# A decoder layer on one core: w_out and value products spread over more heads, the first up chunk converted within the attention, the MoBA keys turned later

## The chip, the cores and the metric

The kernel runs on one core of one Trainium2 chip. The metric is the device time of one execution in microseconds; the profile's span leaves out a little at its ends. TensorE (PE) multiplies and transposes, PEld is its weight load, VectorE (DVE), ScalarE (ACT) and GpSimd (POOL) do the elementwise work, and SyncE (SP) issues nearly all DMAs. Each engine executes its own instructions in order and waits on semaphores.

## What is computed

One layer on 512 tokens of width 1024, all float32:

```
u = rms_norm(x);  proj = u @ w_in            # 416 latent columns, then q, k, v of MoBA, 512 each
MLA:  8 heads, q and k of 64 + 32 rotary, v of 64, from low-rank latents, causal softmax
MoBA: 8 heads of 64, rotary q and k; own block of 256 keys causal, past blocks by top-3 gate
mix = [MLA heads, MoBA heads];  h = x + rms_norm(mix @ w_out) * g
a = square(relu(rms_norm(h) @ w_up))         # 4096 wide
out = h + rms_norm(a @ w_down) * g
```

With two blocks in all, MoBA's selection takes every past block, so its heads are plain causal attention too.

## The kernel before, in words

**Precision.** Every matrix product is made of float32r parts: an operand is split into a high part (ScalarE, `hi_part`, L439) and a low part (VectorE, `lo_part` L710 or with a gain `lo_scaled` L713), and `mm3` (L1029) issues three matmuls: high x high, high x low, low x high. A weight chunk of 1 MB lands in one of two `raw` slots, ScalarE writes its high part, VectorE its low part; `w_ready` counts the finished chunks. Chunks are numbered: 0 to 9 for the input side, 10 to 13 for w_out (`OUT_CH`), 14 and 15 the first two of w_up (`UP_CH`), and so on. SP asks for a chunk when the one two before it has been converted (`chunk`, L248). w_out's chunks are converted in pieces of 512 columns (`out_piece`): the high part by ScalarE (L585), the low part by GpSimd (L380), and four of the sixteen low parts by VectorE (L894).

**Stages.** The input projection goes by column groups of w_in: latents, MoBA q, MoBA k. Its third group (L1185) already holds the transposes for heads 0 and 1 and the scores of head 0. Then comes the loop over 16 heads in `for i in range(NH + 2)`, written out on each of four engines. In step i, TensorE (L1261) computes the scores of head i, makes the first filler (`filler(i, 0)`), the weighted sum of head i-2, transposes the probabilities of head i-1 (`first_T`), makes the second filler, a query or key transpose for a later head, and the rest of the transposes (`last_T`). A filler is two of a unit's `mm3`: the MoBA values (steps 0 to 7, `V_HALVES`), and the half of w_out's product that goes over the MLA rows (steps 10 to 17, `OUT_UNITS`); steps 8 and 9 have none. All use bank 5, which ScalarE empties (`v_part` L576, `out_part` L580) into v_moba or y_part.

Per head the other engines do this. VectorE takes four row maxima (`maxes`, L844), ScalarE the exponentials with their sums (`exps`, L548), VectorE two reciprocals (`inverse_sums`, L856), GpSimd multiplies the probabilities by them (L407 to L411, "normalizing"), TensorE transposes, ScalarE and VectorE split the transposed probabilities in three parts (`p_part`, banks 3, 4 and 3 again), and after the weighted sum ScalarE copies and VectorE adds the two halves of a head (`o_part`). GpSimd splits the sum of each pair of heads (`split_pair`, L387). Of the queries, head i+2's is transposed in step i (`Q_LATE`), a pair of keys in steps 1, 3 and 5 (`K_EARLY`), both for MoBA in steps 6, 8, 10, 12 (`MOBA_PREP`), all in bank 7 (`PREP`). The keys of MoBA are turned (rotary) by VectorE (`swapped` L790, two multiplications of 256 columns; `turned` L804, one of 512) and GpSimd (`rope_add` L366) in step 0: two tiles before the maxima of head 0, two behind. Step 0 ends for ScalarE and VectorE with weight chunk 9 (`in_hi(7)`, `in_lo(7)`).

w_out's pieces stand in steps 6 to 9 (`OUT_PIECES`, L229): on ScalarE and VectorE before `o_part`, on GpSimd at the start of the next step, before the normalizing.

**Behind the heads.** TensorE computes the rest of w_out's product (L1289 to L1312): four token tiles of two halves, 32 `mm3`; then it transposes tile after tile of the new rows and multiplies with w_up in halves of the tokens (L1323 to L1336). ScalarE and VectorE first convert the two up chunks (L643 to L646, L946), which SP asked for behind the four h rows and the gain (L291 to L296). Then, tile by tile, VectorE adds y_part (`added`, L949), ScalarE takes squares, GpSimd the root, VectorE scales and adds the residual (`scaled`, L958), and the transposed rows are split (`transposed_lo`, L728).

The few lines that set the order on SP:

```
L291  sp.wait_ge(o_full, NH)
L292  for t in range(NT):
L293      sp.dma_start(h_sb[:, t, :], x_v[t]).then_inc(h_in[t], 16)
L294  sp.dma_start(post_g[:, :], attn_post_g.to_broadcast([P, D])).then_inc(g_post_in, 16)
L295  for j in range(2):
L296      chunk(UP_CH + j, w_up_v[:, :, 256 * j:256 * j + 256], CW)
```

## Time and profile before

| | |
|---|---|
| median of 3 runs | 642.06 us (641.32 to 642.21) |
| profiled execution, its own time | 643.8 us |
| its span | 641.9 us |
| TensorE busy | 599.7 us, 93% |
| VectorE busy | 309.7 us, 48% |
| ScalarE busy | 281.8 us, 44% |
| GpSimd busy | 113.1 us, 18% |
| chain that ended last | TensorE 81%, VectorE 7%, ScalarE 6%, DMA 2% |
| mean granted TensorE clock | 0.966 |

The page says where time goes by engine. Matmuls overlap and their ends are modelled, so the busy time of TensorE is a little generous: the distance between the starts of two matmuls tells its pace. Three parts follow each other on the time axis: the input projection up to about 92 us, the heads up to 239 us, the transition to the MLP up to 295 us, and the MLP.

### The profile page before, as it was taken

The numbers are of one execution on the slowest core, as the hardware profiler recorded it, in microseconds if no ns is written. First come the engines' busy times: TensorE is split into PE (matmuls) and PEld (weight loads), VectorE is DVE, ScalarE is ACT, GpSimd is POOL, SyncE is SP. The second block draws the span as 40 slices with busy tenths as digits, with TensorE's granted clock in tenths as the row PEclk, the third lists the DMA queues.
The fourth block names the chain that finished last, engine by engine and source line by source line (L and its number), as shares of the span: only waits on it lengthen the run. The fifth ranks groups of instructions, "written<-read, shape, count | busy, mean of one in ns | idle before, by whom it ended". The sixth has DMA issues, their size and how long they took to land.

```text
span 641.9 us, 8151 instructions
## 1 busy us (share of the span) xinstructions
PE 599.7 (93%) x2916; PEld 506.1 (79%) x2916; DVE 309.7 (48%) x596; ACT 281.8 (44%) x581; POOL 113.1 (18%) x173
## 2 busy tenths in 40 slices
PE   8999998998699989369999999999999999999996
PEld 7989877886578877269888888888888888888885
DVE  4478486776656531762543443434242323242435
ACT  5746445667746643236442435353323131322232
POOL 1414153448744520112000000000000000000001
PEclk9999997999679999679999999999999999999999
DMA  8414311001200017400323233332332323222203
GB/s 307 115 61 140 123 66 65 2 1 65 67 0 1 2 36 260 131 1 1 102 94 110 86 98 98 87 109 74 124 131 66 123 73 105 91 92 104 98 1 131
DMA packets 32828, 55.24 MB, mean 86 GB/s; under 512 B 3233, under 2 KB 21409, under 8 KB 32801
## 3 DMA queue, kind: packets, MB, share of 16 engines
q1 hardware_dynamic: 31760, 54.90, 25.7%
q8 instruction: 15, 0.25, 0.2%
q10 hardware_dynamic: 1040, 0.00, 0.1%
q14 instruction: 13, 0.10, 0.0%
HBM read 52.80 MB, written 2.10 MB: 86 GB/s over the span
## 4 chain that ended last, share of the span: by engine, by line
PE 81%; DVE 7%; ACT 6%; DMA 2%; issue 2%; SPq 1%; POOL 0%; DVEq 0%; POOLq 0%; ACTq 0%
PE bank L1031 25%; PE bank L1033 24%; PE bank L1032 24%; PE bank L1190 2%; DVE w_lo L714 2%; ACT probs L557 2%; DMA w_raw<-in_w_up 2%; ACT w_hi L440 1%; PE bank L1224 1%; PE bank L1223 1%; DMA x_sb<-in_x 1%; DVE pT_lo L711 1%; ACT junk_post L465 1%; PE bank L1133 1%; DVE un L964 1%
## 5 line engine op out<-in xcount | busy, mean ns | idle before, releaser
L1031 PE MATMUL bank<-uT_hi,w_hi 128*128 128x512 f32 (+1 forms) x280 | 105.3, 376 | 5.1 <-DVE uT_lo L711 5.1
L1032 PE MATMUL bank<-uT_lo,w_hi 128*128 128x512 f32 (+1 forms) x280 | 105.0, 375 | 0.0
L1033 PE MATMUL bank<-uT_hi,w_lo 128*128 128x512 f32 (+1 forms) x280 | 105.0, 375 | 0.0
L1031 PE MATMUL bank<-w_hi,a_hi 128*128 128x512 f32 x256 | 99.8, 390 | 0.1
L1033 PE MATMUL bank<-w_hi,a_lo 128*128 128x512 f32 x256 | 99.7, 390 | 0.0
L1032 PE MATMUL bank<-w_lo,a_hi 128*128 128x512 f32 x256 | 99.7, 390 | 0.0
L711 DVE TENSOR_TENSOR w_lo<-w_raw,w_hi 128x2048 fp32r<-128x2048 f32 (+2 forms) x21 | 42.6, 2036 | 106.6 <-ACT w_hi L440 106.6
L440 ACT ACTIVATE w_hi<-w_raw 128x2048 fp32r<-128x2048 f32 (+2 forms) x25 | 36.5, 1490 | 111.7 <-PE bank L1033 110.9
L714 DVE SCALAR_TENSOR_TENSOR w_lo<-w_raw,g_up,w_hi 128x256 fp32r<-128x256 f32 x128 | 52.0, 481 | 46.6 <-ACT w_hi L440 46.6
L341 POOL TENSOR_SCALAR stat<-stat 128x1 f32<-128x1 f32 x8 | 1.7, 218 | 374.6 <-ACT junk_post L465 374.6
L1031 PEld LDWEIGHTS bank<-uT_hi,w_hi 128*128 128x128 f32 x280 | 53.8, 192 | 14.4 <-issue 5.5
L675 ACT ACTIVATE relu<-bank 128x512 f32<-128x512 f32 x32 | 19.1, 598 | 98.2 <-PE bank L1033 98.2
L1032 PEld LDWEIGHTS bank<-uT_lo,w_hi 128*128 128x128 f32 x280 | 53.9, 192 | 9.0
L1033 PEld LDWEIGHTS bank<-uT_hi,w_lo 128*128 128x128 f32 x280 | 53.9, 192 | 9.0
L1031 PE MATMUL bank<-w_hi,uT_hi 128*128 128x512 f32 (+1 forms) x144 | 57.8, 402 | 0.6 <-DVE v_moba L890 0.4
L440 ACT ACTIVATE w_hi<-w_raw,g_up 128x256 fp32r<-128x256 f32 x128 | 52.6, 497 | 10.8 <-DMA w_raw<-in_w_up 10.8
L410 POOL TENSOR_TENSOR probs<-probs,rs 128x512 f32<-128x512 f32 (+1 forms) x64 | 46.8, 753 | 56.1 <-DVE rs L862 56.1
L1031 PEld LDWEIGHTS bank<-w_hi,a_hi 128*128 128x128 f32 x256 | 48.1, 188 | 10.5 <-issue 0.5
L1032 PEld LDWEIGHTS bank<-w_lo,a_hi 128*128 128x128 f32 x256 | 48.1, 188 | 10.0
L1033 PEld LDWEIGHTS bank<-w_hi,a_lo 128*128 128x128 f32 x256 | 48.1, 188 | 9.8
L1033 PE MATMUL bank<-w_hi,uT_lo 128*128 128x512 f32 (+1 forms) x144 | 55.6, 386 | 0.0
L1032 PE MATMUL bank<-w_lo,uT_hi 128*128 128x512 f32 (+1 forms) x144 | 55.5, 386 | 0.0
(149 smaller groups left out, 968.3 us busy)
## 6 DMA issues: line engine op xcount, KB each, us to landing
w_raw<-in_w_up SPq DMA_DIRECT2D x16, 1024.0 KB, 5.3
w_raw<-in_w_down SPq DMA_DIRECT2D x16, 1024.0 KB, 4.8
w_raw<-in_w_in SPq DMA_DIRECT2D x6, 1024.0 KB, 5.8
w_raw<-in_w_out SPq DMA_DIRECT2D x4, 1024.0 KB, 4.9
x_sb<-in_x SPq DMA_DIRECT2D x8, 256.0 KB, 6.0
h_sb<-in_x SPq DMA_DIRECT2D x4, 512.0 KB, 5.5
out<-h_sb SPq DMA_DIRECT2D x8, 256.0 KB, 2.0
w_raw<-in_w_in SPq DMA_DIRECT2D x2, 416.0 KB, 5.2
```

Source lines behind the costliest of these rows:

```text
L410: nc.gpsimd.tensor_tensor(pr, pr, rs[:, i % 2, t:t + 1].to_broadcast([P, P * (t + 1)]), ALU.mult).then_inc(s_norm, 1)
L440: return nc.scalar.activation(out, whole, ACT.Copy, scale=scale)
L465: nc.scalar.activation(junk[:, 0:src.shape[1]], src, ACT.Square, scale=scale, accum_out=stat[:, norm, t, col:col + 1]).then_inc(sq, 1)
L557: nc.scalar.activation(probs[i % 2][:, p_off(t):p_off(t) + n], ps[b][:, c:c + n], ACT.Exp, bias=nb[:, i % 2, t:t + 1], scale=-1.0, accum_o ...
L675: nc.scalar.activation(relu[:, m, :], ps[2 * j + m][:, :], ACT.Relu).then_inc(relu_c, 1)
L711: return nc.vector.tensor_tensor(out, whole, hi.bitcast(F32), ALU.subtract)
L714: return nc.vector.scalar_tensor_tensor(out=out, in0=whole, scalar=scale, in1=hi.bitcast(F32), op0=ALU.mult, op1=ALU.subtract)
L964: nc.vector.scalar_tensor_tensor(out=y, in0=y, scalar=stat[:, 3, t, 3:4], in1=post_g[:, w], op0=ALU.mult, op1=ALU.mult).then_inc(y_s, 1)
L1031: nc.tensor.matmul(out, lh, rh, start=start, stop=False)
L1032: nc.tensor.matmul(out, lh, rl, start=False, stop=False)
L1033: return nc.tensor.matmul(out, ll, rh, start=False, stop=stop)
L1190: last = nc.tensor.transpose(ps[b][:, c + P * (t - k):c + P * (t - k) + P], probs[i % 2][:, p_off(t) + P * k:p_off(t) + P * k + P], ident[ ...
```

## The change

- **Fillers.** The sixteen quarters of the value units stand at both halves of steps 0 to 5, then at (6, 1), (7, 1), (8, 1) and (9, 0); those of w_out's units from (10, 1) to (17, 1), and one behind the loop. A quarter is two `mm3`. ScalarE empties w_out's units between the second and the third exponential of a head (`OUT_DONE`).
- **Pieces of w_out.** ScalarE's stand in steps 5, 6, 8 and 9, VectorE's in 8 and 9, both at the end of the step; GpSimd's stand behind the normalizing in steps 6, 7 and 9, and two at the start of step 10.
- **First up chunk.** It has tiles of its own, `up0_hi` and `up0_lo`, where the natural MoBA queries and keys were. SP asks for both up chunks before the h rows. ScalarE and VectorE convert the first in four pairs of 256 columns at the ends of steps 13 to 16; the second is converted behind the heads, as before.
- **Query of head 2.** Transposed in the projection's third group, in bank 3; before it was step 0's late query in bank 7. The key part of heads 2 and 3 waits for ScalarE's copies of bank 7 instead of that query.
- **Turning of the MoBA keys.** One tile in each of steps 1 to 4: the swap between the two reciprocals, the multiplication behind them, GpSimd's addition behind the normalizing. `rt2` has a place of its own.
- **After the heads.** VectorE adds tiles 0 and 1 before it scales tile 0, and so on. `o_part` stays before the probabilities' split ("the sum still ahead of the next transposes").

The diff, cut to what the prediction speaks of:

```diff
-        Q_LATE = {i: i + 2 for i in range(HEADS - 2)}
+        Q_LATE = {i: i + 2 for i in range(1, HEADS - 2)}
-        V_HALVES = range(0, 2 * NT)
-        OUT_UNITS = range(NH + 2 - 2 * NT, NH + 2)
+        V_AT = {(i, half): 2 * i + half for i in range(6) for half in range(2)}
+        V_AT.update({(6, 1): 12, (7, 1): 13, (8, 1): 14, (9, 0): 15})
+        V_DONE = {2: 0, 4: 1, 6: 2, 10: 3}
+        OUT_AT = {((u + 21) // 2, (u + 21) % 2): u for u in range(4 * NT - 1)}
+        OUT_DONE = {11 + u: u for u in range(2 * NT - 1)}
+        TURNED = {1 + t: NT + t for t in range(NT)}
-        OUT_PIECES = {6 + c: [PIECES * c + n for n in range(PIECES)] for c in range(4)}
+        OUT_PIECES = {i: [PIECES * c + n for n in range(PIECES)] for c, i in enumerate((5, 6, 8, 9))}
         DVE_PIECES = {8: (8, 9), 9: (12, 13)}
+        POOL_PIECES = {6: (0, 1, 2, 3), 7: (4, 5, 6, 7), 9: (10, 11), 10: (14, 15)}
+        UP0_PIECES = {13 + n: (2 * n, 2 * n + 1) for n in range(4)}
...
+            for j in range(2):
+                chunk(UP_CH + j, w_up_v[:, :, 256 * j:256 * j + 256], CW)
+
             sp.wait_ge(o_full, NH)
             for t in range(NT):
                 sp.dma_start(h_sb[:, t, :], x_v[t]).then_inc(h_in[t], 16)
             sp.dma_start(post_g[:, :], attn_post_g.to_broadcast([P, D])).then_inc(g_post_in, 16)
-            for j in range(2):
-                chunk(UP_CH + j, w_up_v[:, :, 256 * j:256 * j + 256], CW)
...
             for i in range(NH + 1):
+                for n in POOL_PIECES.get(i, ()) if i == 10 else ():
+                    out_piece(n)
                 if i >= 4 and i % 2 == 0:
                     split_pair(i // 2 - 2)
-                for n in OUT_PIECES.get(i - 1, []):
-                    if n not in DVE_PIECES.get(i - 1, ()):
-                        out_piece(n)
...
+                if i in TURNED:
+                    rope_add(TURNED[i])
+                for n in POOL_PIECES.get(i, ()) if i != 10 else ():
+                    out_piece(n)
...
                 if i < NH:
-                    exps(i, S_ORDER)
+                    exps(i, S_ORDER[:2])
+                if i in OUT_DONE:
+                    out_part(OUT_DONE[i])
+                if i < NH:
+                    exps(i, S_ORDER[2:])
                 if i == 0:
+                    q_part(2, 3)
                     natural(NT + 2)
...
-                for n in OUT_PIECES.get(i, []):
-                    out_piece(n)
                 if i >= 2:
                     o_part(i - 2)
...
+                for n in OUT_PIECES.get(i, []):
+                    out_piece(n)
+                if i in UP0_PIECES:
+                    up0_pieces(UP0_PIECES[i])
...
-            for j in range(2):
-                act.wait_ge(*SLOT_LEFT[UP_CH + j][0])
-                mlp_hi(j, UP_CH + j)
+            act.wait_ge(*SLOT_LEFT[UP_CH + 1][0])
+            mlp_hi(1, UP_CH + 1)
...
-                if i == 0:
-                    turn_two(NT)
...
                     maxes(i, S_ORDER)
-                    inverse_sums(i)
+                    inverse_sums(i, 0)
+                    if i in TURNED:
+                        swapped(TURNED[i])
+                    inverse_sums(i, 1)
                 if i == 0:
-                    turn_two(NT + 2)
+                    q_part(2, 3)
                     in_lo(7)
+                if i in TURNED:
+                    turned(TURNED[i])
...
-            for j in range(2):
-                mlp_lo(j, UP_CH + j)
+            mlp_lo(1, UP_CH + 1)
...
+            added(0)
+            added(1)
+            dve.wait_ge(g_post_in, 16)
+            post_norm(0)
+            added(2)
+            post_norm(1)
+            transposed_lo(2 * NT, 0)
+            transposed_lo(2 * NT, 1)
+            added(3)
+            post_norm(2)
+            post_norm(3)
+            transposed_lo(2 * NT, 2)
+            transposed_lo(2 * NT, 3)
...
+                elif (part, t) == (1, 3):
+                    pe.wait_ge(qup_c, 2 * NT)
+                    q_prep(2, 3)
...
                 if i in K_EARLY:
-                    pe.wait_ge(ql, i + 2)
+                    pe.wait_ge(*((nat_c, 2 * NT) if i == 1 else (ql, i + 2)))
                     k_prep(K_EARLY[i], PREP)
...
-            pe.wait_ge(w_ready, UP_CH + 2 - NO)
+            pe.wait_ge(w_ready, UP_CH + 1 - NO)
             pe.wait_ge(ul, 2 * NT + 4)
-            up_block(0, 0, 0, A)
+            up_block(0, 0, 0, A, (up0_hi, up0_lo))
...
+            pe.wait_ge(w_ready, UP_CH + 2 - NO)
             up_block(2, 1, 0, A)
```

## Rows read from the trace of the kernel before

**Rows 1.** The page's slices of 16 us: TensorE's busy tenths, and its granted clock.

```profile
PE   8999998998699989369999999999999999999996
...
PEclk9999997999679999679999999999999999999999
```

**Rows 2.** Windows, one per step: length, busy us (count) by engine, granted clock, DMA, GB/s.

```profile
92.68:105.53 12.85, 9.67 (x44) 7.93 (x42) 9.72 (x19) 5.28 (x14) 5.61 (x6) 0.73 0.24 82
...
130.15:138.94 8.79, 8.33 (x53) 7.19 (x50) 6.02 (x17) 6.33 (x16) 3.63 (x6) 1.00 0.00 0
138.94:148.70 9.76, 8.11 (x53) 7.06 (x51) 6.28 (x18) 7.83 (x19) 6.59 (x8) 1.00 0.01 2
148.70:157.42 8.72, 7.39 (x44) 6.17 (x44) 5.07 (x16) 6.27 (x17) 6.04 (x8) 1.00 0.35 120
157.42:167.70 10.28, 6.15 (x40) 4.87 (x39) 8.30 (x20) 7.82 (x19) 10.28 (x10) 0.86 0.31 102
167.70:178.09 10.39, 8.20 (x32) 6.87 (x31) 6.65 (x17) 6.38 (x16) 6.33 (x8) 0.64 0.01 3
178.09:189.46 11.37, 11.37 (x51) 9.53 (x51) 5.41 (x16) 4.90 (x14) 6.14 (x7) 0.70 0.00 0
189.46:196.92 7.46, 7.46 (x44) 6.12 (x43) 4.83 (x15) 5.05 (x14) 3.69 (x6) 1.00 0.00 0
196.92:205.13 8.21, 8.21 (x52) 7.02 (x51) 5.38 (x16) 5.38 (x15) 3.75 (x5) 1.00 0.01 2
```

**Rows 3.** Windows of the idle time in step 8 and of the stretch behind the heads.

```profile
163.90:167.08 3.18, 0.26 (x4) 0.02 (x2) 3.18 (x5) 3.05 (x6) 3.18 (x5) 0.65 0.85 267
239.17:295.02 55.85, 38.78 (x201) 33.71 (x200) 27.44 (x50) 19.50 (x45) 4.77 (x14) 0.85 0.36 121
255.50:267.14 11.64, 0.15 (x1) 0.00 (x1) 9.46 (x22) 3.74 (x10) 1.01 (x3) 0.71 0.58 180
```

**Rows 4.** Timelines behind the heads (start, us, what, idle before); the h rows' landing.

```profile
251.30 6.50 ACT L440 ACTIVATE w_hi<-w_raw,g_up 128x256 fp32r<-128x256 f32 x16 [10.82 <-DMA w_raw<-in_w_up]
...
254.64 6.45 DVE L714 SCALAR_TENSOR_TENSOR w_lo<-w_raw,g_up,w_hi 128x256 fp32r<-128x256 f32 x16 [13.43 <-ACT w_hi L440]
261.00 1.28 DVE L956 TENSOR_TENSOR un<-bank,y_part 128x512 f32<-128x512 f32 x2
264.47 1.41 DVE L964 SCALAR_TENSOR_TENSOR un<-un,stat,post_g 128x512 f32<-128x512 f32 x2 [2.18 <-POOL stat L345]
265.80 1.29 DVE L969 TENSOR_TENSOR h_sb<-un,h_sb 128x512 f32<-128x512 f32 x2
...
DMA to landing us min/median/max: 4.3/5.5/6.2
```

**Rows 5.** Timelines of VectorE and TensorE at the start of the heads.

```profile
80.07 2.74 DVE L714 SCALAR_TENSOR_TENSOR w_lo<-w_raw,g_in,w_hi 128x512 fp32r<-128x512 f32 x4 [1.65 <-ACT w_hi L440]
82.73 1.43 DVE L799 TENSOR_TENSOR rt<-mk_nat,rope_sb 128x256 f32<-128x256 f32 x4
...
88.84 1.31 DVE L799 TENSOR_TENSOR rt<-mk_nat,rope_sb 128x256 f32<-128x256 f32 x2 [0.40 <-ACT mk_nat L440]
...
92.97 4.39 DVE L714 SCALAR_TENSOR_TENSOR w_lo<-w_raw,g_in,w_hi 128x512 fp32r<-128x512 f32 x4 [0.32 <-ACT w_hi L440]
...
98.02 0.80 PE L1031 MATMUL bank<-cT_hi,wkv_hi 128*128 128x512 f32 x1 [3.18 <-DVE qT_lo L711]
```

**Rows 6.** GpSimd's forms by cost, a row of ScalarE's timeline, and waits within the heads.

```profile
L410 POOL TENSOR_TENSOR probs<-probs,rs 128x512 f32<-128x512 f32 x15 | 15.6, 1041 | 53.0 <-DVE rs L862 53.0
...
L385 POOL TENSOR_TENSOR wo_lo<-w_raw,wo_hi 128x512 fp32r<-128x512 f32 x8 | 10.0, 1276 | 0.0
...
144.28 2.21 ACT L440 ACTIVATE wo_hi<-w_raw 128x512 fp32r<-128x512 f32 x4
...
DVE rs L862 <- ACT probs L557: 16.4, 15, 1.1
...
PE bank L1031 <- ACT y_part L583: 2.2, 2, 1.1
```

More of the change, by code:

```diff
@@ L590, in out_piece, with up0_pieces @@
                 hi_part(out_tiles(c)[0][:, w], raw[OUT_CH[c] % 2][:, w]).then_inc(wo_hi_ready, 1)
+            def up0_pieces(pair):
+                if pair[0] == 0:
+                    act.wait_ge(g_up_in, 16)
+                    arrived(UP_CH)
+                for k in pair:
+                    w = slice(256 * k, 256 * k + 256)
+                    last = hi_part(up0_hi[:, w], raw[UP_CH % 2][:, w], g_up[:, k:k + 1])
+                last.then_inc(up0_h, 1)
             k_part(0, 0)
@@ L932, in _ @@
                     k_part(MOBA_PREP[i], PREP)
+                for n in DVE_PIECES.get(i, ()):
+                    out_piece(n)
+                if i in UP0_PIECES:
+                    up0_pieces(UP0_PIECES[i])
             dve.wait_ge(last_h, 1)
@@ L1287, in _ @@
                     last_T(i - 1)
+            out_quarter(4 * NT - 1)
             def out_final(t, b, ks):
```

139 lines of the change are left out of this document (65 added, 74 removed).

## The prediction

> **What bounds the kernel now.** First the page's slices: of 40, TensorE is at nine tenths or more in all but eight; the low ones are slices 7, 10, 11, 15, 17 and 18 (16 us each), and the granted clock is down in 7, 11, 12, 17 and 18 [rows 1]. Behind them the MLP keeps TensorE busy up to the last slice. TensorE's work is the same in both kernels, so the change is worth what it takes out of those dips. I call "step i" the stretch from the first score matmul of head i to that of head i+1. By step [rows 2], a step in which TensorE never idles takes 7.46 us (head 11) or 8.21 us (head 12, with a query and a key transposed as well). Heads 1 and 6 to 10 take far longer: 12.85, 9.76, 8.72, 10.28, 10.39 and 11.37, three of them at a granted clock of 0.64 to 0.86. Near the end of the heads TensorE waits twice for the copy of y_part, 1.1 us each [rows 6]. Then the attention is over at 239.17 and the stretch up to the end of the first three part blocks of the MLP (295.02) takes 55.85 us [rows 3]. Its work is 32 products of 0.683 us (three matmuls of 512 columns at 0.2275 from start to start), four groups of transposes of 0.81 and three half blocks of 2.95: 33.9 us. 11.64 us of the difference are idle in one piece [rows 3].
>
> Times behind the heads count from the end of the last filler, T0 = 239.17.
>
> **The transition, after T0.** Before, VectorE gets both up chunks first: ScalarE waits 10.82 us for the DMA and converts from 251.30 to 257.8, VectorE ends at 261.09, and only then adds tile 0, at T0+21.8, though its 8 products had been ready at T0+5.5 (8 x 0.683) [rows 4]. After, the DMA sits inside the attention, one chunk is converted there, and one remains: ScalarE T0+0.7 to +4.0 (half of 6.50), VectorE +4.0 to +7.2 (half of 6.45). On SP's queue the two chunks move ahead of the h rows and wait there for raw slots that GpSimd's and VectorE's w_out pieces free, in my walk by the middle of the heads; so they block nothing, and the h rows are asked for after the last weighted sum, as before. Those landed in 4.3 to 6.2 us [rows 4], the gain behind them a little later, so all by about T0+9, before the first norm at +12.2. Now each step of VectorE, with durations of [rows 4]:
> - Sum 0 (1.28): +7.2 to 8.5. Its norm could start at +10.7, 2.2 after the sum (ScalarE's squares, GpSimd's root). Sum 1 needs tile 1's products (T0+10.9): ends +12.2. Norm 0 (1.41+1.29, together 2.62) ends +14.9. TensorE is in tile 2 until +16.4 and finds the rows for the transposes ready.
> - Sum 2 ends +17.0, norm 1 +19.6; TensorE wants it at +20.0 after half of tile 3. No wait.
> - TensorE ends tile 3 at +23.5 (32 x 0.683 + 2 x 0.81). The low parts of tiles 0 and 1 are ready at about +22.5. First block to +26.5. Sum 3 ends +24.1, norm 2 +26.7: a wait of 0.3. Then transposes, block, transposes, block, with norm 3 at +29.4, ready: end at +34.2.
> So 55.85 becomes 34.2: **21.6 us**. The order "sum 1 before norm 0" makes norm 0 1.5 us later; that is hidden under tile 2's products, and costs 1.5 if they end early. The first block needs only the chunk from the heads, so the second chunk's conversion hides under all of tiles 0 to 3. TensorE's new wait for the second chunk stands before the third block, 24 us after it is ready.
>
> **The start, heads 0 to 5.** In step 1 before, TensorE idles 3.18 us up to 98.02 because it waits for head 2's query in bank 7; VectorE has turned four tiles of the MoBA keys and then took 4.39 us for a chunk that took 2.74 at 80.07 [rows 5]. After, the query is transposed and split during the projection. The key part of head 2 waits for the natural copies alone, ready at 90.7. The filler's second weight chunk: ScalarE 90.7 to 93.2, VectorE 2.74 more, 95.95; TensorE gets there at 95.5, an idle time of 0.5, and the clock has no reason to fall. It was at 99.47 before and then ran at half (matmuls 0.43 us apart instead of 0.23). New is this: VectorE has maxes (1.8), a turn (1.4), key parts (1.39) and the probabilities' low part between that and the transposes of head 0, and TensorE waits about 1.8 us before the late query. Scores of head 2 then start at 102.3 instead of 105.53: **3.2 us**. In heads 2 to 5 the turn of one tile per head costs VectorE 2 x 0.36 and one more of 512 columns, about as much: 1.4 us [rows 5], put into two waits it has anyway: 1.1 us for the exponentials before the second reciprocal, [rows 6] and that for the key's high part behind them. GpSimd's additions (1.46 us each) stand behind its normalizing, where it waits some 3 us for the next head. If the cover were gone, four turns would cost 5.6 us. Steps 3 and 5 stay at 8.8 us, step 2 and 4 at 7.7: 0.4 us more.
> Against it speaks that the turn reads two SBUF tiles while GpSimd normalizes. The row: with GpSimd at work the pair of multiplications took 1.31 us instead of 0.72 (half of 1.43), and the chunk 4.39 instead of 2.74 [rows 5]. From +0.2 to +0.6 for a pair and as much for the other multiplication, partly hidden: I take 1.0 us off for all four heads, bounds 0 and 3.
> If instead each of the three VectorE operations of a turn waited out one of GpSimd (1.04 us the longest [rows 6]), four heads would lose 3 x 1.04 x 4 = 12.5 us: the second rival. The Trainium skill ("SBUF — State Buffer", section "SBUF: two separate sides") states that rule: VectorE with two SBUF inputs and GpSimd share a port pair by an exclusive lock for a whole instruction. The trace shows it only in part.
>
> **Heads 6 to 11.** Before, heads 8 and 9 have no filler, and ScalarE does four pieces of w_out (2.2 us) ahead of the sum and the probabilities, GpSimd four (4 x 1.276 = 5.1 us) ahead of the normalizing [rows 6]. TensorE waits for all of them, and the clock halves: by the means of 0.86, 0.64 and 0.70 in steps 8, 9 and 10, for about 2.9 + 7.5 + 6.8 = 17 us [rows 2]. Half of that, 8.6 us, is lost where TensorE had work. After, every one of heads 6 to 10 has one quarter (1.4 us), and pieces come last. My walk by the durations of these steps, with head 6 at 0 (before: 9.76, 18.48, 28.76, 39.15, 50.52 for heads 7 to 11, 57.98 for head 12):
> - Step 6: the pieces of head 5 hold the last third of the probabilities back by about 1.5, TensorE waits for the queries' low part; 9.2.
> - Step 7: pieces of head 6 in the same place; 8.0. TensorE has one transposing pair and 1.4 us of filler less than in a full step, so ScalarE binds: 1.2 (last third) after the scores, maxes, exponentials 2.15, sum 0.6 and 0.7, low part 0.6, transposes, back to the scores.
> - Step 8: nothing in the way; TensorE's own work, 6.6.
> - Step 9: pieces of head 8 on ScalarE, two on VectorE; TensorE idle 2.7; 9.1.
> - Step 10: the same from head 9, v_moba's last tile too; 9.3. GpSimd, with 5.0 + 1.9 + 5.0 ahead, ends the normalizing 3.6 us before TensorE needs it.
> - Step 11: 7.4.
> Sum 49.6 instead of 57.98: **8.4 us**.
>
> **Heads 12 to the end.** The two waits of 1.1 to 1.3 for the copy of y_part go, since half a step now lies between a unit and the next: 2.6. One quarter more is left to do: -1.4. Two pieces of the up chunk per head 13 to 16 take ScalarE 0.95 and VectorE 0.8, most of it in ScalarE's 0.9 us of waiting for the last third of the transposes; -0.5 for four, bounds 0 and 2. **0.7 us**.
>
> **Sum.** 3.2 + 0.4 - 1.0 + 8.4 + 0.7 = 11.7, and 21.6: 33.3 us. The profiled execution took 643.8, so 610.5; the runs' median (642.06) is 1.7 lower, and so is my forecast: **608.8**. The MLP behind has TensorE without idle time before and should keep it. What a measurement of this kernel can tell from no change is about 0.2% (1.3 us).
>
> **Rivals.**
> - *Clock falls once or twice in steps 9 to 11.* Before, TensorE was idle 3.18 us up to 98.02 and nearly so from 163.90 to 167.08, and its clock was down in both places [rows 3, 5]; mine are 2.7 and at most 1.8. One stretch of some 7 to 10 us at the lower level (1.2 GHz) costs half its length where TensorE is full: 612 to 614. Chance 0.23.
> - *The turns pay the full price of GpSimd's operations*: 12.5 instead of 1.0, 620.3. It decides once turns outgrow their 2 us of cover; then VectorE binds steps 1 to 4. For it: VectorE's pair went from 0.72 to 1.31 beside GpSimd. Against it: the chunk of four operations was stretched by 1.65 and not by four times 1.04 [rows 5], and VectorE is busy for 6.0 of 8.8 us in step 5 [rows 2], which leaves room. 0.08.
> - *The early chunks do nothing*, because slot 1 comes free late or the sums stay chained behind the conversion; 642.1 - 11.7 = 630.4. Against it: the last out piece is done by head 10. 0.04.
> - *Slower.* One quarter per head is so little that TensorE's clock stays at half from head 6 to the last head. There TensorE has some 83 us of work at full clock; at half it takes 75 us more than my 91: about 684. It decides from the point where the halved stretches hold over 67 us of matmuls. Against it: step 7 with TensorE busy for 7.39 of 8.72 us kept a clock of 1.00 [rows 2]. 0.03.
> The forecast itself: 0.60, its own range 605.5 to 612; 0.02 for what is none of these. The range leaves out the last three: 604.5 to 615. Faster 0.96, same 0.01, slower 0.03.
>
> **What would show it.** Right: no idle of 11 us behind the last head, the sums start some 7 us after it; the stretch of 55.85 is under 36. Scores of head 2 near 102, of head 12 near 186; the first half-clock stretch of the attention gone. Wrong: granted clock below 1 in steps 9 to 11; turns of over 2 us beside GpSimd; a wait of ScalarE for the up chunk; TensorE waiting for h_sb before its last transposes.

## The result, and the profile after

The changed kernel takes 618.29 us (median of 4 runs, 617.81 to 618.97), the kernel before 641.79 beside it (641.32 to 642.21). The ratio is 0.9635, with an interval of 0.9618 to 0.9651. The forecast was 608.8 with a range of 604.5 to 615.0: the direction was right, the size was not, and the time lies 3.3 us above the range. Of the 33.3 us that the steps promised, 23.5 came by the medians and 26.0 by the profiled executions (643.8 to 617.81; its span 616.0). The execution of before that was profiled was one of its long ones: all runs of that kernel in this study lie between 640.1 and 645.0, those of the changed one between 617.5 and 619.0.

The page's slices of the changed kernel, now 15.4 us each, TensorE's busy tenths and its granted clock:

```profile
PE   7999998998799999999999999999999999999996
...
PEclk9999999997969999999999999999999999999999
```

Five slices are under nine tenths, the first, 7, 10, 11 and the last, where [rows 1] had eight; the clock is down in 10 and 12 alone. The deep dips, of 3 and 6 tenths behind the heads and of 6 in steps 8 and 9, are gone.

The windows by step (columns as in [rows 2]), from step 1 to the end of the last filler, and last the stretch up to the end of the first three part blocks:

```profile
92.88:102.61 9.73, 7.49 (x43) 5.75 (x41) 9.04 (x21) 5.16 (x15) 3.98 (x5) 1.00 0.29 108
...
127.00:135.82 8.82, 8.33 (x53) 7.19 (x50) 6.17 (x18) 6.42 (x17) 4.85 (x7) 1.00 0.00 0
135.82:145.08 9.26, 7.22 (x46) 5.88 (x46) 6.28 (x18) 7.67 (x20) 4.51 (x6) 1.00 0.01 2
145.08:154.06 8.98, 8.98 (x39) 8.08 (x38) 5.44 (x16) 6.29 (x17) 8.32 (x9) 0.62 0.32 117
154.06:161.12 7.06, 7.06 (x45) 5.87 (x44) 4.96 (x15) 5.12 (x14) 3.78 (x4) 1.00 0.28 85
161.12:172.95 11.83, 7.57 (x38) 5.95 (x37) 6.38 (x18) 7.11 (x19) 7.84 (x11) 0.85 0.11 41
172.95:182.78 9.83, 9.83 (x46) 8.44 (x45) 8.39 (x19) 6.82 (x18) 9.75 (x10) 0.66 0.65 209
182.78:190.55 7.77, 7.62 (x43) 6.11 (x42) 4.87 (x16) 5.16 (x14) 3.31 (x6) 1.00 0.01 5
...
206.86:214.95 8.09, 7.62 (x43) 6.12 (x42) 6.07 (x17) 5.38 (x16) 4.43 (x6) 1.00 0.00 0
...
234.56:269.17 34.61, 34.17 (x201) 30.04 (x200) 23.58 (x41) 15.80 (x36) 8.10 (x14) 1.00 0.35 122
```

Steps 2 and 4 and steps 3 and 5 are alike, so 127.00 stands for step 5; head 12 starts at 190.55, and T0 is 234.56. Where the time went, against the forecast:

| stretch | before | forecast | after |
|---|---|---|---|
| head 6's first score | 138.94 | 2.6 less | 135.82, 3.1 less |
| steps 6 to 11 | 57.98 | 49.6 | 54.73 |
| head 12 to T0 | 42.25 | 0.7 less | 44.01 |
| T0 to three part blocks | 55.85 | 34.2 | 34.61 |
| from there to the end of the span | 346.9 | the same | 346.8 |

The two ends are right within half a microsecond; 7.6 us are missing in the middle, of which 5.1 in steps 6 to 11 and 2.5 from head 12 on. The stretch of steps 6 to 11 has the clock at half for as long as before, 17 us: 6.8 in step 7 (from 145.4) and 10.2 in steps 9 and 10 (from 169.3). The fall in step 1 is gone.

VectorE's timeline behind T0 (columns as in [rows 4]):

```profile
238.58 3.25 DVE L733 SCALAR_TENSOR_TENSOR w_lo<-w_raw,g_up,w_hi 128x256 fp32r<-128x256 f32 x8 [3.94 <-ACT w_hi L448]
241.75 1.88 DVE L985 TENSOR_TENSOR un<-bank,y_part 128x512 f32<-128x512 f32 x3
245.64 0.69 DVE L985 TENSOR_TENSOR un<-bank,y_part 128x512 f32<-128x512 f32 x1 [2.01 <-PE bank L1069]
246.25 1.40 DVE L993 SCALAR_TENSOR_TENSOR un<-un,stat,post_g 128x512 f32<-128x512 f32 x2
```

VectorE finishes the second chunk and adds tile 0 at T0+7.2, where [rows 4] had T0+21.8, and scales it at +11.7. The second half of tile 1 waits 2.01 us for its products, so what sets the time is TensorE's products, as the forecast had it.

Then GpSimd's and TensorE's timelines around step 9:

```profile
165.03 0.61 POOL L403 CAST uT_hi<-o_sum 128x512 fp32r<-128x512 f32 x1 [7.19 <-PE bank L1069]
...
166.94 5.45 POOL L417 TENSOR_TENSOR probs<-probs,rs 128x512 f32<-128x512 f32 x8
...
169.74 1.54 PE L1229 MATMUL bank<-ident,probs 128*128 128x128 f32 x6 [3.65 <-POOL probs L417]
```

GpSimd stands idle for 7.19 us, and what it waits for is a matmul. Then it normalizes heads 8 and 9 back to back (8 tiles), and TensorE idles 3.65 us until it has done so. The second half of step 8, with nothing in GpSimd's hands to do, is where head 8's normalizing should have been. `split_pair(2)` (L401) waits not only for the sum of its heads but for all four value units, since for the third pair the split goes over rows that the value fillers still read:

```
pool.wait_ge(*((qup, 2 * NT) if c < 2 else (proj, 4 * NT)))
```

The change moved the last value quarter to (9, 0), into the step behind the one in which GpSimd asks for it. Behind that instruction stands the normalizing of head 8, for which TensorE waits.

Last, rows of VectorE's and GpSimd's timelines that show single prices:

```profile
98.01 1.59 DVE L818 TENSOR_TENSOR rt<-mk_nat,rope_sb 128x256 f32<-128x256 f32 x2
...
113.85 0.74 DVE L818 TENSOR_TENSOR rt<-mk_nat,rope_sb 128x256 f32<-128x256 f32 x2
...
206.95 1.90 DVE L733 SCALAR_TENSOR_TENSOR up_lo<-w_raw,g_up,up_hi 128x256 fp32r<-128x256 f32 x2
...
215.12 0.88 DVE L733 SCALAR_TENSOR_TENSOR up_lo<-w_raw,g_up,up_hi 128x256 fp32r<-128x256 f32 x2
...
207.08 1.49 POOL L405 TENSOR_TENSOR uT_lo<-o_sum,uT_hi 128x512 fp32r<-128x512 f32 x1
```

A turn's swap beside GpSimd takes 1.59 us against 0.74 where it starts ahead of GpSimd's operation (113.85 against 114.01); an up piece pair takes 1.90 beside GpSimd's split and 0.88 otherwise.

### The profile page after: what moved, and what is told of

Same layout as the page of the kernel before. It is cut to its first block, busy times and chain, and to the rows that moved or that the text cites. A ratio compares the mean times of both kernels' runs of the same rounds, so it can differ in the third digit from the quotient of the medians.

```text
span 616.0 us, 8166 instructions
## 1 busy us (share of the span) xinstructions
PE 593.9 (96%) x2916; PEld 499.8 (81%) x2916; DVE 310.7 (50%) x596; ACT 282.5 (46%) x581; POOL 116.5 (19%) x173
## 4 chain that ended last, share of the span: by engine, by line
PE 86%; DVE 5%; ACT 4%; issue 2%; DMA 1%; POOL 1%; SPq 0%; DVEq 0%; POOLq 0%; ACTq 0%
PE bank L1067 27%; PE bank L1069 26%; PE bank L1068 26%; PE bank L1229 2%; ACT probs L565 2%; DVE pT_lo L730 1%; PE bank L1263 1%; PE bank L1262 1%; DMA x_sb<-in_x 1%; PE bank L1169 1%; DVE w_lo L733 1%; DVE o_sum L902 1%; ACT w_hi L448 1%; PE bank L1073 1%; PE bank L1109 1%
## 5 line engine op out<-in xcount | busy, mean ns | idle before, releaser
L1067 PE MATMUL bank<-uT_hi,w_hi 128*128 128x512 f32 (+1 forms) x248 | 94.9, 383 | 0.0
L1068 PE MATMUL bank<-uT_lo,w_hi 128*128 128x512 f32 (+1 forms) x248 | 94.8, 382 | 0.0
L1069 PE MATMUL bank<-uT_hi,w_lo 128*128 128x512 f32 (+1 forms) x248 | 94.8, 382 | 0.0
L733 DVE SCALAR_TENSOR_TENSOR w_lo<-w_raw,g_up,w_hi 128x256 fp32r<-128x256 f32 x120 | 48.8, 480 | 37.1 <-ACT w_hi L448 37.1
L1024 DVE TENSOR_TENSOR act_sb<-relu 128x512 f32 (+1 forms) x32 | 22.1, 689 | 64.6 <-ACT relu L694 64.6
L1069 PEld LDWEIGHTS bank<-uT_hi,w_lo 128*128 128x128 f32 x248 | 46.6, 188 | 9.1
L1067 PEld LDWEIGHTS bank<-uT_hi,w_hi 128*128 128x128 f32 x248 | 46.6, 188 | 9.1
L1068 PEld LDWEIGHTS bank<-uT_lo,w_hi 128*128 128x128 f32 x248 | 46.6, 188 | 8.9
```

Of the source, the lines that this page charges most:

```text
L733: return nc.vector.scalar_tensor_tensor(out=out, in0=whole, scalar=scale, in1=hi.bitcast(F32), op0=ALU.mult, op1=ALU.subtract)
L1024: nc.vector.tensor_tensor(act_sb[:, bass.ds(i * 4 + (2 * j + m), 1), :], relu[:, m:m + 1, :], relu[:, m:m + 1, :], ALU.mult).then_inc(a_re ...
L1067: nc.tensor.matmul(out, lh, rh, start=start, stop=False)
L1068: nc.tensor.matmul(out, lh, rl, start=False, stop=False)
L1069: return nc.tensor.matmul(out, ll, rh, start=False, stop=stop)
```

## The experiments

Three questions were open. First, whether the loss in steps 6 to 11 is the wait of `split_pair(2)`, or whether the clock falls there by itself, because the steps hold too little work for TensorE. Second, what the conversion of the up chunk costs in the heads, and what it buys. Third, how much of the gain each of the forecast's parts really is. Each kernel below is the changed kernel with one edit, if nothing else is said; ratios are to the kernel before, timed beside it. One thing bears on several of the comparisons: in the profiled executions of the changed kernel step 7 takes 8.98 us, with a fall of the clock, and in those of the first, third, fourth, fifth and sixth variant below it takes 8.20, without one, though their edits touch nothing that this step waits for. Of their differences from the changed kernel 0.8 us is therefore owed to no edit, as far as the profiled execution stands for the others.

### The split behind the normalizing

```diff
-                if i >= 4 and i % 2 == 0:
+                if i >= 4 and i % 2 == 0 and i != 8:
                     split_pair(i // 2 - 2)
...
+                if i == 8:
+                    split_pair(2)
```

> The changed kernel, with GpSimd's split of the third pair of heads put behind the normalizing of head 8 instead of ahead of it. Theory A (in the changed kernel GpSimd waits 7.2 us at that split, for the last value quarter in step 9, and head 8's normalizing stands behind it; TensorE then idles 3.65 us for it and the clock halves): the idle time goes, step 9 falls from 11.8 to about 9 and step 10 from 9.8 to about 9.0, the clock stays at 1.00 in both; 613.5 to 615 us. Rival B (step 9 is long because ScalarE's and VectorE's w_out pieces of step 8 hold back the last third of head 7's probabilities): step 9 stays near 11.8 and the time at 618. Rival C (the clock falls because steps 6 to 10 have too little work): the idle time goes but the clock still reads below 1 in steps 9 or 10; 616 us.

Measured: 614.58 us (614.52 to 614.91), 0.9563 (0.9537 to 0.9589), 3.7 less than the changed kernel. GpSimd's timeline, of this kernel:

```profile
157.73 2.76 POOL L417 TENSOR_TENSOR probs<-probs,rs 128x512 f32<-128x512 f32 x4
164.17 0.61 POOL L403 CAST uT_hi<-o_sum 128x512 fp32r<-128x512 f32 x1 [3.68 <-PE bank L1071]
...
166.09 2.75 POOL L417 TENSOR_TENSOR probs<-probs,rs 128x512 f32<-128x512 f32 x4
```

Head 8 is normalized at 157.73, ahead of the wait, and head 9 at 166.09. The wait itself, still 3.68 us, stands behind work that is done. The windows of steps 9 and 10:

```profile
160.28:168.75 8.47, 6.23 (x37) 5.11 (x37) 6.29 (x18) 7.21 (x19) 4.71 (x7) 1.00 0.21 85
168.75:179.44 10.69, 9.73 (x46) 8.11 (x45) 9.10 (x19) 6.61 (x18) 10.49 (x11) 0.68 0.61 196
```

Step 9 falls from 11.83 to 8.47. But step 10 rises from 9.83 to 10.69: there the clock is at half for 6.8 us from 170.2. So the wait is the cause of the loss in step 9. It is worth 2.5 us in steps 9 and 10 together (21.66 to 19.16); most of the rest of the 3.7 is the 0.8 of step 7. What is left of a low clock has another cause.

### All value fillers before step 8

The values go back to both halves of steps 0 to 7, as before, w_out's to steps 10 to 17, and the copy of each unit ahead of all exponentials of a head.

```diff
-        V_AT = {(i, half): 2 * i + half for i in range(6) for half in range(2)}
-        V_AT.update({(6, 1): 12, (7, 1): 13, (8, 1): 14, (9, 0): 15})
-        V_DONE = {2: 0, 4: 1, 6: 2, 10: 3}
-        OUT_AT = {((u + 21) // 2, (u + 21) % 2): u for u in range(4 * NT - 1)}
+        V_AT = {(i, half): 2 * i + half for i in range(8) for half in range(2)}
+        V_DONE = {2: 0, 4: 1, 6: 2, 8: 3}
+        OUT_AT = {((u + 20) // 2, (u + 20) % 2): u for u in range(4 * NT)}
```

> The changed kernel with the fillers where they were (values in steps 0 to 7, w_out from step 10 on, none in 8 and 9, each unit emptied ahead of the exponentials); the pieces, the early chunk, the early query and the turns stay changed. Theory A: the values are done in step 7, so the split of the third pair does not wait and head 8's normalizing is early, but TensorE has no filler in steps 8 and 9: it idles there and the clock may halve; steps 12 to 17 come back to 7.46 us with two waits of 1.1 at the end. I expect 616 to 620, so the spreading is worth next to nothing. If spreading is worth what I forecast (about 5 us of the 8.4 in steps 6 to 11): 622 to 624.

Measured: 615.36 us (614.07 to 618.27), 0.9567 (0.9537 to 0.9597). Windows of steps 8 to 11 of this kernel, with edges within 0.1 us of the steps' own:

```profile
156.40:165.30 8.90, 8.76 (x39) 7.61 (x38) 5.71 (x17) 5.74 (x15) 8.82 (x10) 0.62 0.36 118
165.30:173.70 8.40, 4.95 (x31) 3.97 (x30) 6.48 (x18) 7.13 (x19) 3.41 (x6) 1.00 0.01 4
173.70:185.10 11.40, 11.40 (x52) 9.56 (x51) 7.99 (x18) 6.05 (x17) 9.97 (x10) 0.70 0.57 184
185.10:192.50 7.40, 7.40 (x43) 6.07 (x42) 4.82 (x15) 5.01 (x14) 3.67 (x6) 1.00 0.00 0
```

Here GpSimd's split has no value filler to wait for. Steps 8 and 10 run at 0.62 and 0.70, and yet the kernel is 2.9 us faster than the changed one, and only 0.8 slower than the one with the split behind, which has its fillers spread. So the fillers over more heads brought 0.8 us at most, which the two intervals cannot tell from nothing, and they made the wait. (The profiled execution is the longest of the four, 618.27; it has a fall of the clock in step 2, which takes 10.59 us instead of 7.78.) With the copy ahead of the exponentials steps 11 to 13 take 7.46, 8.23 and 7.46 us, as in the kernel before, and 7.77, 8.55 and 7.76 in the changed one: the copy between the exponentials costs 0.3 us in each. The pieces stand as in the changed kernel, and steps 7 to 11 take 45.0 us against 48.2 [rows 2]: that gain comes without the spread fillers.

### The first up chunk behind the heads

```diff
-                if i in UP0_PIECES:
-                    up0_pieces(UP0_PIECES[i])
...
+            for pair in UP0_PIECES.values():
+                up0_pieces(pair)
```

The same on ScalarE and VectorE, ahead of the second chunk.

> The changed kernel with the first up chunk converted behind the heads, after the last split of the sums and ahead of the second chunk; both are still asked for before the h rows. Theory: ScalarE and VectorE take 3.3 us more each before sum 0, so sum 0 starts at about +10.5 instead of +7.2, norm 0 ends at about +16 to +17 (sum 0, sum 1 at +13, norm 0), about when TensorE reaches its transposes (+16.4), norm 1 at +21 to +22 against the +20.0 TensorE wants it: 1 to 3 us lost, and about 1 us won in steps 14 to 16. 618 to 621. Rival: the early conversion is what gave the 21 us: 628 or more.

Measured: 616.50 us (616.32 to 616.66), 0.9592 (0.9565 to 0.9618): 1.8 us faster than the changed kernel. VectorE's timeline behind T0 (232.31), of this kernel:

```profile
233.93 3.28 DVE L733 SCALAR_TENSOR_TENSOR up_lo<-w_raw,g_up,up_hi 128x256 fp32r<-128x256 f32 x8 [1.54 <-ACT up_hi L448]
239.53 3.26 DVE L733 SCALAR_TENSOR_TENSOR w_lo<-w_raw,g_up,w_hi 128x256 fp32r<-128x256 f32 x8 [2.32 <-ACT w_hi L448]
```

And its windows, from head 15 to T0 and from there to the three part blocks:

```profile
214.12:232.31 18.19, 18.04 (x100) 15.18 (x99) 8.82 (x22) 9.62 (x22) 4.64 (x6) 1.00 0.09 30
232.31:266.90 34.59, 34.09 (x198) 29.50 (x197) 26.77 (x49) 18.60 (x44) 7.42 (x14) 1.00 0.35 122
```

The transition is nearly as long as in the changed kernel, though VectorE has both chunks to do, because TensorE has 32 products to make meanwhile. The first block starts 24.0 us behind T0 instead of 23.6 and the third at 32.0 instead of 31.7; the window's edge at 266.90 lies 0.4 us ahead of the end of the third. Step 14 and what follows up to T0 take 1.84 us less (25.87 against 27.70). So converting the chunk within the heads costs 1.8 us and buys 0.4. That the whole run gains 1.8 and not 1.4 fits the shorter step 7.

### The chunks asked for behind the h rows

The edit before, and SP asks for the up chunks where the kernel before did:

```diff
             sp.dma_start(post_g[:, :], attn_post_g.to_broadcast([P, D])).then_inc(g_post_in, 16)
+            for j in range(2):
+                chunk(UP_CH + j, w_up_v[:, :, 256 * j:256 * j + 256], CW)
```

> The kernel with the first chunk converted behind the heads (e3_chunk_behind), and with both up chunks asked for behind the h rows and the gain, as before. Theory D (the gain of the transition comes from the earlier request: the 10.8 us that ScalarE waits for the DMA): the first chunk lands near +12, both are converted by +22, sum 0 starts there as in the kernel before; TensorE idles 10 us ahead of its transposes and the clock falls; 12 to 15 us more than e3_chunk_behind, 628 to 632. Rival (the new order of sums and norms hides most of it): 620 to 623.

Measured: 628.34 us (627.18 to 629.27), 0.9766 (0.9747 to 0.9784), 11.8 more than the kernel above. Timelines of ScalarE and VectorE, of this kernel (T0 is 234.07):

```profile
244.35 3.31 ACT L447 ACTIVATE up_hi<-w_raw,g_up 128x256 fp32r<-128x256 f32 x8 [9.49 <-DMA w_raw<-in_w_up]
...
250.90 3.25 DVE L732 SCALAR_TENSOR_TENSOR w_lo<-w_raw,g_up,w_hi 128x256 fp32r<-128x256 f32 x8 [2.32 <-ACT w_hi L447]
254.07 2.48 DVE L984 TENSOR_TENSOR un<-bank,y_part 128x512 f32<-128x512 f32 x4
```

ScalarE waits 9.49 us for the DMA, VectorE is through with the chunks 20 us behind T0, and TensorE's first part block starts at +35.2 instead of +24.0. By the profiled executions 10.8 us of the difference lie behind T0 and 1.2 in step 2, where the clock falls and which the edit does not touch. The earlier request alone is worth some 11 us.

### Norms in turn

```diff
-            added(0)
-            added(1)
-            dve.wait_ge(g_post_in, 16)
-            post_norm(0)
-            added(2)
-            post_norm(1)
...
+            for t in range(NT):
+                added(t)
+                if t == 0:
+                    dve.wait_ge(g_post_in, 16)
+                if t >= 2:
+                    transposed_lo(2 * NT, t - 2)
+                post_norm(t)
+            for t in range(2, NT):
+                transposed_lo(2 * NT, t)
```

> The changed kernel with VectorE's order behind the heads as before: sum, norm, sum, norm, with the low parts of tiles 0 and 1 behind sums 2 and 3. Theory (the order matters, because the first up block waits for the low parts of tile 1, which then stand behind sum 3): sum 0 at +7.2, norm 1 ends at +19.4, norm 2 at +25.5, low part of tile 1 at about +28; the first block starts there instead of at +23.6, so 4 to 5 us more, 622 to 623.5. Rival (all of the transition's gain comes from the earlier chunks, the order is free, as the forecast's text had it for sum 1 and norm 0): 618 to 619.

Measured: 623.48 us (623.11 to 623.79), 0.9693 (0.9677 to 0.9709), 5.2 more than the changed kernel. VectorE's timeline, of this kernel (T0 is 234.98):

```profile
258.14 1.41 DVE L993 SCALAR_TENSOR_TENSOR un<-un,stat,post_g 128x512 f32<-128x512 f32 x2
...
260.67 1.28 DVE L985 TENSOR_TENSOR un<-bank,y_part 128x512 f32<-128x512 f32 x2
261.87 1.28 DVE L730 TENSOR_TENSOR uT_lo<-bank,uT_hi 128x512 fp32r<-128x512 f32 x2
```

The low part of tile 1, which the first part block needs, stands behind the sum of tile 3 at 261.87. The first block starts at +28.3 instead of +23.6, and the clock falls for 3.4 us at 263.2. The order of the sums is worth 5 us.

### The turning of the keys in step 0

```diff
-        TURNED = {1 + t: NT + t for t in range(NT)}
+        TURNED = {}
```

With the swaps, multiplications and additions back in step 0; the third query stays early.

> The changed kernel with all four MoBA key tiles turned in step 0, as before; head 2's query stays early. Theory: VectorE ends the second value chunk near 97.4 instead of 96, TensorE's idle time ahead of the filler of step 1 is 2 us instead of 0.67, but the wait of 1.5 us ahead of head 3's query goes; scores of head 2 start at 103 to 104 instead of 102.6; the time is 0.5 to 1.5 us longer than the changed kernel, 619 to 620. Rival (the early query alone, not the turn, or the reverse, gave the 3 us at the start): without the turn's move the scores of head 2 start at 105 or later and the clock halves, 621 or more.

Measured: 619.22 us (619.0 to 619.37), 0.9632 (0.9606 to 0.9659), 0.9 more than the changed kernel. TensorE's timeline, of this kernel:

```profile
97.76 0.50 PE L1082 MATMUL bank<-w_hi,uT_hi 128*128 128x512 f32 x1 [2.17 <-DVE w_lo L739]
```

TensorE waits 2.17 us for the filler's weight chunk and has the scores of head 2 at 104.1 instead of 102.61, and those of head 6 at 137.24 instead of 135.82: the turns' move is worth 1.4 us at the start. The other 1.7 of the 3.1 are left for the query by subtraction; no run has the query late and the turns moved.

### The sum behind the next probabilities

```diff
-                if i >= 2:
-                    o_part(i - 2)
...
+                if i >= 2:
+                    o_part(i - 2)
```

On ScalarE and VectorE, from before the probabilities' split to behind its first two parts.

> The changed kernel with the sum of a head's two halves (ScalarE's copy 0.58, VectorE's addition 0.68) behind the first two splits of the transposed probabilities instead of ahead of them. Theory E (in steps 11 to 15 and in steps 3 and 5 the last transposes wait 0.3 to 0.7 us for VectorE's low part, because the sum is ahead of it): steps 3 and 5 fall from 8.8 to about 8.2, steps 11 to 15 from 7.8 to 7.5; 3 to 4 us less, 614.5 to 616. Rival (the sum is wanted soon itself, by the next weighted sum or by GpSimd's split): no change or slower, 618 to 620.

Measured: 619.61 us (618.16 to 621.28), 0.9640 (0.9615 to 0.9664). Windows of steps 3, 4, 11 and 14 and of the stretch from head 15 to T0, of this kernel:

```profile
110.50:118.66 8.16, 8.16 (x52) 7.24 (x51) 7.23 (x20) 5.77 (x15) 5.77 (x7) 1.00 0.01 2
118.66:127.10 8.44, 7.67 (x49) 6.60 (x48) 7.67 (x21) 5.28 (x14) 6.03 (x8) 1.00 0.01 2
181.72:189.13 7.41, 7.41 (x43) 6.19 (x43) 4.27 (x14) 5.17 (x14) 2.80 (x4) 1.00 0.00 0
204.76:213.25 8.49, 7.91 (x43) 6.07 (x42) 6.51 (x17) 5.38 (x16) 4.33 (x6) 1.00 0.00 0
213.25:235.68 22.43, 19.89 (x99) 16.57 (x99) 13.00 (x29) 11.99 (x28) 5.14 (x7) 0.92 0.08 28
```

Steps 3 and 5 fall from 8.83 to some 8.1 and steps 11 to 13 to 7.4, 8.2 and 7.4 (before the edit 7.77, 8.55, 7.76). Step 4 rises from 7.78 to 8.44 and step 14 from 8.09 to 8.49, so that head 15 starts only 1.7 us earlier, 213.25 instead of 214.95. The stretch to T0 takes 22.43 instead of 19.6, 2.8 more, with the clock at 0.92. There a pair of VectorE's up pieces takes 2.32 us beside GpSimd's split of the pair, 1.90 in the changed kernel. The low part of the last third of the probabilities stands behind it, and TensorE's weighted sum idles 2.06 us for that. So the last heads lose more than the others gain, and the whole, 1.3 us more, is within the spread of its runs.

### Three edits together

The split behind the normalizing, the first up chunk behind the heads, and the sum behind the probabilities.

> Three changes at once on the changed kernel: GpSimd's split of the third pair behind the normalizing, the first up chunk converted behind the heads, the sum behind the first two splits. If their effects add (3.7, 1.8 and 3 to 4 us): 609 to 610. If the clock falls again in steps 9 or 10 as in e1_split_behind: 611 to 612.

Measured: 610.64 us (610.34 to 610.99), 0.9496 (0.9480 to 0.9512): 7.6 us less than the changed kernel. Alone the three gave 3.7, 1.8 and -1.3. The first two make 5.5, so in this company the sum's place gives 2.1. Windows of steps 9, 10 and 11 and of the stretch to T0, of this kernel:

```profile
159.13:166.99 7.86, 6.23 (x38) 5.10 (x37) 5.90 (x17) 6.59 (x18) 5.17 (x9) 1.00 0.34 130
166.99:178.38 11.39, 9.17 (x46) 7.76 (x45) 9.72 (x20) 7.67 (x19) 11.09 (x11) 0.70 0.56 185
178.38:185.80 7.42, 7.42 (x44) 6.22 (x43) 4.35 (x15) 5.18 (x14) 2.80 (x4) 1.00 0.00 0
208.80:226.78 17.98, 17.98 (x99) 15.23 (x99) 9.17 (x23) 9.63 (x22) 4.71 (x6) 1.00 0.09 32
```

With no up pieces in the way the sum's place costs nothing at the end: 17.98 us to T0, where the kernel with the chunk behind the heads has 18.19 and the changed one 19.6; and there is no wait in steps 11 to 14. What is left is step 10, 11.39 us at a clock of 0.70, half from 169.3 for 6.8 us.

What holds step 10 stands in the same trace. VectorE's w_out pair of step 8 and of step 9, and GpSimd's four pieces:

```profile
160.25 1.31 DVE L732 TENSOR_TENSOR w_lo<-w_raw,w_hi 128x512 fp32r<-128x512 f32 x2
167.91 3.25 DVE L732 TENSOR_TENSOR w_lo<-w_raw,w_hi 128x512 fp32r<-128x512 f32 x2
167.66 5.87 POOL L396 TENSOR_TENSOR w_lo<-w_raw,w_hi 128x512 fp32r<-128x512 f32 x4
```

Beside GpSimd's pieces the pair takes 3.25 us instead of 1.31. Behind it stand the low part of head 8's last third (171.08) and that of the last value tile (171.42), and TensorE idles 2.22 us until 172.25 for its weighted sum. No run parts the two engines' pieces in this place, so what it would bring is not shown.

### What the low clock costs

To the last kernel, 70 matmuls of 128 columns are added, 30 in step 9 ahead of the last transposes and 40 in step 10 ahead of the weighted sum of head 8, where TensorE waits. They compute nothing that is used.

```diff
+                if i == 9:
+                    pe.wait_ge(kl, k_preps(10))
+                    for _ in range(30):
+                        nc.tensor.matmul(ps[PREP][:, 0:P], ident_b[:, :], ident_b[:, :], start=True, stop=True)
...
+                if i == 10:
+                    pe.wait_ge(o_both, 8)
+                    for _ in range(40):
+                        nc.tensor.matmul(ps[O][:, 0:P], ident_b[:, :], ident_b[:, :], start=True, stop=True)
```

> On e8_three: 30 matmuls of 128 bf16 columns into the free bank 7 ahead of head 8's last transposes, 40 into the free bank of the weighted sums ahead of head 8's own sum; they compute nothing that is used and lie where TensorE waits 2.1 and 2.8 us. Theory G (the clock halves in step 10 for these waits and the stretch of 6.8 us costs about 2.5 us): the clock stays at 1.00, step 10 falls from 11.4 to about 9, 608 to 608.5 us. Rival (the lower clock is hidden, since ScalarE and VectorE bind these steps): 610 to 611.

Measured: 609.35 us (609.20 to 609.40), 0.9480 (0.9454 to 0.9506), the fastest of all, though the interval overlaps that of the three edits alone. Step 10 of this kernel:

```profile
166.93:177.27 10.34, 9.70 (x85) 8.12 (x85) 8.84 (x19) 7.48 (x19) 10.26 (x10) 1.00 0.54 169
```

The clock stays at full through all heads, and yet step 10 takes 10.34 us: the 6.8 us at half cost only 1.0 to 1.3 us. The weighted sum starts 5.3 us into the step in both kernels, at either clock, because it waits for VectorE's low parts; the added matmuls are over 0.3 us before it. Only what comes behind runs shorter. So in step 10 the low clock is mostly an effect and not a cause.

### Two attempts at step 10 that missed

Both begin from the three edits together. The first spreads the pieces of w_out over steps 5 to 10, and VectorE's and GpSimd's with them (VectorE's in steps 7 and 9, GpSimd's last in step 11):

```diff
-        OUT_PIECES = {i: [PIECES * c + n for n in range(PIECES)] for c, i in enumerate((5, 6, 8, 9))}
+        OUT_PIECES = {5: (0, 1, 2, 3), 6: (4, 5, 6, 7), 7: (8, 9), 8: (10, 11), 9: (12, 13), 10: (14, 15)}
```

> On e8_three: w_out's last eight pieces over steps 7 to 10, two per step on ScalarE (VectorE's pair of step 8 in step 7, GpSimd's last pair at the start of step 11) instead of four in step 8 and four in step 9. Theory F (after GpSimd's wait, what binds steps 9 and 10 is ScalarE's 2.2 us of pieces plus VectorE's two, which hold back the last third of the probabilities and v_moba): TensorE's waits of 2.1 us in step 9 and 2.8 us in step 10 fall to 1 to 1.5, step 7 grows by about 0.7, and the clock may keep 1.00 in step 10; 607 to 609 us. Rival (the work is only moved and every step it goes to grows by as much): 610.5 to 612.

Measured: 616.38 us (616.02 to 617.92), 0.9588 (0.9562 to 0.9615), 5.7 more than without it. ScalarE's timeline and the window of step 8, of this kernel:

```profile
154.20 1.15 ACT L450 ACTIVATE w_hi<-w_raw 128x512 fp32r<-128x512 f32 x2 [1.95 <-DMA w_raw<-in_w_out]
```

```profile
152.30:164.70 12.40, 9.68 (x45) 8.24 (x44) 8.40 (x19) 6.06 (x16) 9.02 (x9) 0.72 0.37 130
```

The earlier pieces ask for a chunk that has not landed: ScalarE waits 1.95 us for the DMA. VectorE's pair behind it falls beside GpSimd's four pieces and takes 2.54 us, and head 6's last low part stands behind the pair, so that TensorE idles 2.73 us. Step 8 takes 12.4 us instead of 6.83, and the clock is at half three times instead of once.

The second begins w_out's fillers half a step earlier, as before the change, so that none is left behind the loop:

```diff
-        OUT_AT = {((u + 21) // 2, (u + 21) % 2): u for u in range(4 * NT - 1)}
+        OUT_AT = {((u + 20) // 2, (u + 20) % 2): u for u in range(4 * NT)}
```

The copy stands ahead of all exponentials again.

> On e8_three: w_out's sixteen quarters one place earlier, from (10, 0) to (17, 1) as in the kernel before, none behind the loop, and each unit emptied ahead of the exponentials; the values stay spread. Theory H (a unit's quarter pair straddling two steps puts ScalarE's 0.58 us copy among the exponentials and costs 0.3 us per step with the sum ahead, nothing with the sum behind, where steps 11 to 14 already take 7.40): steps 11 to 14 stay at 7.4, the two waits of 1.1 for the copy come back at the end (2.2 us), one quarter less is left (1.4 less) but step 10 is longer by up to 1.4: 610.5 to 612.5 us. Rival (the first quarter falls into the wait of 2.8 us in step 10 and costs nothing): 609.5 to 610.5.

Measured: 615.36 us (614.11 to 615.55), 0.9572 (0.9541 to 0.9603), 4.7 more. The window of step 10, of this kernel:

```profile
168.00:181.60 13.60, 12.67 (x51) 10.44 (x50) 9.52 (x20) 7.54 (x19) 11.12 (x11) 0.62 0.47 155
```

Step 10 takes 13.60 us and the waits for the copy of y_part in the last heads are back. With the three edits in place, w_out's units later by half a step are right as they are.

### The changed kernel again

> The changed kernel itself again, for its time beside the variants on this chip and for how often step 7 shows the lower clock: in one profile it did (step 7 8.97 us), in three variants with the same code up to there it did not (8.20). 617 to 619 us.

Measured: 618.03 us (617.50 to 618.32), 0.9615 (0.9593 to 0.9638). Its profile has the same steps (7: 8.96, 9: 11.81, 10: 9.89), with the clock at half from 145.4 and 169.3. The fall in step 7 is there in both profiles of this kernel.

## Why the prediction was right and wrong

- **The transition** was right: 21.2 us gained where the forecast had 21.6. Its reasons held too: the request is worth some 11 us and the order of the sums 5; the other 5 have no run of their own. Its one wrong reason is that the chunk from the heads matters here. Without it the first block starts 0.4 us later.
- **The start** was right: head 2's scores at 102.61 (forecast 102.3), an idle time of 0.67 before the filler (0.5), no fall of the clock. The 1.0 us taken off for turns beside GpSimd was not paid: the pair did stretch, to 1.59 us (0.85 more, where 0.2 to 0.6 was foreseen), but steps 2 to 5 took 7.78, 8.83, 7.78 and 8.82, as forecast without it, so none of it reached TensorE.
- **Steps 6 to 11 failed**, 5.1 us of the miss: step 9 is 2.7 over its forecast, step 7 is 1.0 over, 8, 10 and 11 half a microsecond or less each, and step 6 came as forecast (9.26 against 9.2). The step that failed is the walk's item on step 9, "pieces of head 8 on ScalarE, two on VectorE; TensorE idle 2.7; 9.1". It leaves GpSimd out, and the only sentence on GpSimd, in the item on step 10 ("with 5.0 + 1.9 + 5.0 ahead"), counts what that engine has to do and not what it waits for. The wait of `split_pair(2)` for the last value quarter stands in the code of both kernels; before, the quarter came in step 7, in the step before the split, and cost nothing. The wait took 7.19 us, and it cost 2.5 us in steps 9 and 10. The kernel without it takes 614.6, just inside the range, but 0.8 of its gain is step 7, where the clock did not fall; so part of that is luck. In the changed kernel it fell there (8.98 against 8.0), which no step of the walk had.
- **Heads 12 to the end failed** by 2.5 us. The term "-0.5 for four, bounds 0 and 2" was mis-sized: the conversion in the heads costs 1.8 us, since VectorE's pair takes 1.90 beside GpSimd's split and not the 0.8 that I took from rows without it. The bound held it, the value didn't. The remainder, 1.2, is the copy of y_part, now between exponentials: 0.3 us in each step, by the experiment with all value fillers before step 8.
- **The rival of a falling clock** had the clock right and stayed 4 us under the time (612 to 614): the clock was at half for 17 us in steps 7, 9 and 10, as long as in steps 8 to 10 before. But its price, half the length, was wrong: the 6.8 us at half in step 10 of the three edits cost 1.0 to 1.3, and the 6.8 us in step 7 of the changed kernel 0.8 (8.98 against 8.20).
- **The full price of GpSimd's operations** fell, although its 620.3 lies 2 us from the measured time; that is chance, since the steps with turns took no longer. And so did **the early chunks do nothing** and **slower**. Of the early chunks' rival one part is true: the early request is what counts, and the early conversion buys only 0.4.
- **The conversion to a median** took 1.7 us off the profiled execution. The changed kernel's median lies 0.5 above its profiled execution instead, so 2.2 of the 9.5 us between 608.8 and 618.3 are here, and the other 7.3 are 33.3 less 26.0. How far a profiled execution lies from its median is no constant to carry from one kernel to the next.
- **One reading** is wrong without bearing on the sum: of the long steps four and not three are at a granted clock of 0.64 to 0.86, since head 1 has 0.73 [rows 2].

What stays open is why the clock falls in step 7 in both profiles of the changed kernel and in none of the variants with the same code up to there. What would relieve step 10 was tried twice without success; taking VectorE's pair of pieces away from GpSimd's, which the rows of the three edits suggest, was not tried.

## What to carry to other kernels

When work of one engine is moved, list every semaphore that counts it and go through all who wait on it, with what is queued behind each: here one quarter of a filler, moved by two steps, held an engine that has no part in the filler for 7 us. Ask of each part of a change by itself whether its place or its early request brings the gain, since an early conversion that nobody waits for takes time from heads that are full. And before going after a low clock, ask which engine binds that stretch.
